# Weight blocks read in pieces of 16 KB instead of 2 KB, in a block of two transformer layers on one core

## The reference

```python
c_act = jax.nn.silu(c)
ada = c_act @ w_ada[l] + b_ada[l]              # w_ada: 1024 x 3072
shift, scale, gate = jnp.split(ada, 3, axis=-1)
h = rms_norm(x) * (1.0 + scale[:, None, :]) + shift[:, None, :]
p = h @ w_in[l]                                # w_in: 1024 x 3600
...
x = x + gate[:, None, :] * y
```

## Time and profile before

| | us |
|---|---|
| three runs | 2122.72, 2126.60, 2126.88 |
| median | 2126.6 |
| span of the profiled execution, first to last instruction | 2124.1 |
| PE busy in it | 2037.9 (96%) |
| PE busy in its first 60 us | 38.6 |

### The profile page before, as it was taken

How to read it: one execution, slowest core, us unless ns; L and a number is a source line. 1 busy time by engine, 2 the same in 40 slices (tenths; PEclk the granted TensorE clock), 3 DMA queues, 4 the chain that set the end, 5 groups by cost and what they waited for, 6 DMA issues and landing times.

```text
span 2124.1 us, 37932 instructions
## 1 busy us (share of the span) xinstructions
PE 2037.9 (96%) x15636; PEld 1158.4 (55%) x15636; DVE 915.3 (43%) x1510; ACT 573.6 (27%) x1048; POOL 326.1 (15%) x292
## 2 busy tenths in 40 slices
PE   6999999999999999999999999999899999999996
PEld 3486655655334445543456444565566666666653
DVE  2535551555556642886466554244611111111114
ACT  2123322333663210442133221143011111111113
POOL 0214430532330012004000010000100000000003
PEclk9999999999999999999999999999899999999999
DMA  8210311123104026100122102100899999999986
GB/s 317 86 45 25 105 60 60 70 85 104 40 8 151 30 90 153 71 1 0 40 80 81 68 0 80 43 31 40 319 384 410 413 410 411 405 403 410 400 359 244
DMA packets 108971, 346.90 MB, mean 163 GB/s; under 512 B 20216, under 2 KB 59536, under 8 KB 95952
## 3 DMA queue, kind: packets, MB, share of 16 engines
q1 hardware_dynamic: 64272, 274.98, 33.3%
q0 software_dynamic: 14528, 48.51, 6.8%
q10 hardware_dynamic: 30080, 22.18, 3.2%
HBM read 310.77 MB, written 40.24 MB: 165 GB/s over the span
## 4 chain that ended last, share of the span: by engine, by line
PE 86%; DVE 7%; ACT 4%; issue 1%; DMA 1%; POOL 1%; DVEq 0%; ACTq 0%; POOLq 0%; PEldq 0%
PE bank L685 19%; PE bank L1482 16%; PE bank L692 11%; PE bank L840 9%; PE bank L1498 8%; ACT work L1602 3%; PE bank L927 2%; PE bank L866 2%; PE bank L1263 1%; PE bank L1059 1%; PE bank L760 1%; PE bank L1488 1%; PE bank L1473 1%; DVE O L2115 1%; PE bank L1064 1%
## 5 line engine op out<-in xcount | busy, mean ns | idle before, releaser
L685 PE MATMUL bank<-slots,HT 128*128 128x512 f32 (+2 forms) x832 | 295.3, 511 | 1.7 <-DVEq L144 1.1
L1602 ACT ACTIVATE work<-bank 128x512 f32<-128x512 f32 (+6 forms) x227 | 117.4, 522 | 406.1 <-PE bank L685 120.0
L685 PEld LDWEIGHTS bank<-slots,HT 128*128 128x128 f32 x832 | 146.4, 190 | 134.0 <-issue 128.7
L1602 ACT ACTIVATE HT<-bank 64x256 f32<-64x256 f32 (+2 forms) x215 | 92.9, 432 | 433.0 <-PE bank L1482 278.4
L1602 ACT ACTIVATE work<-work 128x1024 f32<-128x1024 f32 (+7 forms) x199 | 158.6, 808 | 169.2 <-DVEq L144 114.4
L1482 PE MATMUL bank<-slots,HT 128*32 128x256 f32 x3136 | 172.4, 379 | 2.2 <-DVE HT L2862 1.3
L2868 DVE TENSOR_TENSOR HT<-HT,bank 64x256 f32<-64x256 f32 x97 | 41.0, 423 | 300.3 <-ACT HT L1602 300.3
L1482 PE MATMUL bank<-work,HT 128*32 128x256 f32 x3072 | 168.7, 379 | 0.0
L2982 POOL TENSOR_TENSOR work<-work 128x1024 f32<-128x1024 f32 (+4 forms) x80 | 120.3, 1504 | 240.8 <-DVEq L144 150.6
L1482 PEld LDWEIGHTS bank<-slots,HT 128*32 128x32 f32 x3136 | 103.1, 110 | 68.5 <-issue 2.9
L1482 PEld LDWEIGHTS bank<-work,HT 128*32 128x32 f32 x3072 | 101.1, 110 | 64.6
(11 more groups left out here) (319 smaller groups left out, 2922.5 us busy)
## 6 DMA issues: line engine op xcount, KB each, us to landing
slots<-in_w_e_gate_dram SPq DMA_DIRECT2D x17, 2048.0 KB, 11.1
slots<-in_w_e_up_dram SPq DMA_DIRECT2D x17, 2048.0 KB, 15.8
slots<-in_w_e_down_dram SPq DMA_DIRECT2D x17, 2048.0 KB, 17.2
work<-in_w_e_gate_dram SPq DMA_DIRECT2D x16, 2048.0 KB, 11.4
work<-in_w_e_up_dram SPq DMA_DIRECT2D x16, 2048.0 KB, 15.9
work<-in_w_e_down_dram SPq DMA_DIRECT2D x16, 2048.0 KB
slots<-in_w_in_dram SPq DMA_DIRECT2D x9, 2048.0 KB, 8.4
slots<-in_w_ada_dram SPq DMA_DIRECT2D x6, 2048.0 KB, 14.8
```

The source lines that it names most:

```text
L685: ins = pe.matmul(bank, lhsT, rhs, start=(n == 0), stop=(n == len(pairs) - 1))
L1602: return act.activation(o, i, f, bias=bias, scale=scale, **more)
```

## The change

The host lays out each block of 512 columns of `w_ada` so that each partition's part (8 row blocks of 512 floats) is one run of 16 KB, as it already does for the experts' weights, and does the same with a copy of the first 512 columns of `w_in`. The kernel loads `ada0` to `ada5` and `a_qk` from there. The place in `slots`, the bytes, the order, the waits and all products stay as they are. `w_in` itself stays as an input for the other blocks.

```diff
+def column_blocks(w, n=HALF):
+
+    return by_partition(np.stack([w[:, at:at + n] for at in range(0, w.shape[1], n)]))
...
-        w_ada, w_in, w_out = (A[n].rearrange("a (k p) n -> p (a k) n", p=P) for n in ("w_ada", "w_in", "w_out"))
+        w_in, w_out = (A[n].rearrange("a (k p) n -> p (a k) n", p=P) for n in ("w_in", "w_out"))
+        w_ada = [cut(A["w_ada"][n], NK) for n in range(6)]
...
         for n in (0, 2):
-            add_chunk(f"ada{n}", (w_ada, 512 * n, 512 * n + 512))
-        add_chunk("a_qk", (w_in, 0, 512))
+            add_chunk(f"ada{n}", (w_ada[n], 0, 512))
+        add_chunk("a_qk", (cut(A["w_in_first"][0], NK), 0, 512))
         for n in (1, 3):
-            add_chunk(f"ada{n}", (w_ada, 512 * n, 512 * n + 512))
+            add_chunk(f"ada{n}", (w_ada[n], 0, 512))
...
-        add_chunk("ada4", (w_ada, 512 * 4, 512 * 5))
+        add_chunk("ada4", (w_ada[4], 0, 512))
...
-        add_chunk("ada5", (w_ada, 512 * 5, 512 * 6))
+        add_chunk("ada5", (w_ada[5], 0, 512))
...
+    arrays["in_w_ada_dram"] = column_blocks(_np.asarray(inputs["w_ada"])[0])
+    arrays["in_w_in_first_dram"] = column_blocks(_np.asarray(inputs["w_in"])[0][:, 0:HALF])
```

More of the change, by code:

```diff
@@ L3316 @@
         arrays[f"in_{name}_dram"] = by_partition(_np.asarray(inputs[name])[0])
+    arrays["in_w_ada_dram"] = column_blocks(_np.asarray(inputs["w_ada"])[0])
+    arrays["in_w_in_first_dram"] = column_blocks(_np.asarray(inputs["w_in"])[0][:, 0:HALF])
     for name, table in zip(("consts", "masks", "packed"), (*constants(), packed(inputs))):
         arrays[f"in_{name}_dram"] = table
-    for name in _INS + ["consts", "masks", "packed"]:
+    for name in _INS + ["w_in_first", "consts", "masks", "packed"]:
         a = arrays[f"in_{name}_dram"]
```

## The result

The changed kernel took 2136.26 us (median of 4 runs, 2134.57 to 2138.82) against 2126.36 for the kernel before. The medians are 9.9 us apart. The ratio over all runs is 1.0052, with a 95% interval of 1.0039 to 1.0065, so by it the kernel is slower by some 11 us (8 to 14). The forecast was 2140.4, range 2133 to 2144. The profiled execution has a span of 2133.6 us, 9.5 more than before.

The account below looks back on a forecast made before the run. PE is busy 96%; early on the chain waits for x, not weights. 16 KB weight packets taking turns with x's 4 KB rows move ACT's pair 1 start from 15.40 to 29.2: 2126.6 + 13.8 = 2140.4 us, range 2133 to 2144.

Parts of the forecast that it names:

- rival A: `ada1` comes late and finds q1 empty, so x is through first: pair 1 at 23.9, +8.5 us, 2135.1; 16%.
- main case: x pair 1 lands at 29.2, behind the three first weight loads and `ada1`: +13.8 us, 2140.4, own range 2137 to 2143; 65%.
- Form and turns: The changed loads really get 16 KB packets, and the engines still take the queues one to one by packet.
- Rival B: x keeps at least half the bandwidth, as engines weigh bytes or cut 16 KB pieces: +1.1 us, 2127.7; 8%.
- x pair 0 near 19.6: x pair 0, 16 turns beside 16 KB packets, lands near 19.6 instead of 11.3.
- `ada0` landing near 8: `ada0` lands near 8 instead of 13.7, but its product waits for silu until about 16.5.
- The small transfers near 16.5, `ada1` issued near 20.1: q10's `packed` and identity land near 16.5, not 8.2; the product with `ada0` ends at 20.0, then SP issues `ada1`.
- `ada1` follows `a_qk` without a gap, pair 1 at 29.2: On q1 `a_qk` ends at 21.8, `ada1` starts near 22.0, ahead of x's last rows; pair 1 lands at 29.2: +13.8 us.
- Everything after hangs in one chain: All work after ACT's start on pair 1 shifts by the same 13.8 us; nothing later gives time back.
- Clock, priced at 0 within 1.6 us: PE's granted clock over the transposes, 0.69 after idleness, starts low again after a longer wait: 0, within 1.6 us.
- Rival C: A gain: x's first packet comes sooner or PE misses a 1.2 GHz stretch; ACT begins 3.3 us sooner, 2123.3; 3%.
- The page of the Trainium skill on small descriptors: Some three cycles of overhead per packet would bring the same bytes 3% sooner, under 1 us; rows showed no such gain.

Follow-up runs that it names:

- extra_load: Changed kernel with one more 2 MB load in 16 KB pieces issued right behind `a_qk`; 2142.10 us, ratio 1.0079 to the kernel before.
- hold_ada1: Changed kernel, but SP issues `ada1` only when x pair 1 has landed; 2134.04 us, ratio 1.0043 to the kernel before.
- pieces_2kb: Changed kernel's layout with 64 unused bytes after every 2 KB, so packets are 2 KB again; 2125.51 us, ratio 1.0002 to the kernel before.
- the additional products: 48 identity products on PE before its first real product, added to both x-first kernels; 2124.62 us (16 KB) and 2126.19 us (2 KB).
- x_first_16kb: Changed kernel, but SP issues x pairs 0 and 1 itself ahead of `ada0`; 2120.60 us, ratio 0.9978 to the kernel before; repeat 2120.07 us.
- x_first_2kb: Kernel before, with x pairs 0 and 1 moved to SP's queue ahead of `ada0`; 2125.80 us, ratio 1.0004 to the kernel before.

## Why the prediction was right, point by point

The direction and the mechanism were right: x loses its turns' worth of bandwidth to the longer packets, and the chain hands the delay on unchanged. One term of the sum was not, and it makes 4.3 us of 13.8: whether `ada1` follows `a_qk` at once. The measured 2136.26 lies inside 2133 to 2144 because that range took in rival A; the main case's own range, 2137 to 2143, begins 0.7 us above it.

- *Form and turns.* Right. 16 KB pieces are one packet, and q0 and q1 sent equal numbers of packets at 2, 4, 8 and 16 KB. Rival B, x keeping half of the bytes, would have given 2127.7. It is refuted by the 272 to 273 packets with 3.93 and 1.05 MB.
- *x pair 0 near 19.6.* It landed at 1.28 + 17.9 = 19.2, so near in part by luck: the engines moved 424 GB/s from 6 to 14 us and not the 400 of the earlier trace rows, and its 16 completions have a mean of 18.4, but the last of them came 0.8 us after that.
- *`ada0` landing near 8.* It landed at 9.7, and nothing waited for it.
- *The small transfers near 16.5, `ada1` issued near 20.1.* ACT started at 16.50, and SP issued at 20.20:

```profile
20.20 17.30 SPq L3238 DMA_DIRECT2D slots<-in_w_ada_dram  x2
```

- *`ada1` follows `a_qk` without a gap, pair 1 at 29.2.* This is the step that failed, and the term that was mis-sized by it. From 21 to 22 us, then from 22 to 23:

```profile
q0 software_dynamic: 85, 0.35, 85.6%
q1 hardware_dynamic: 15, 0.03, 8.5%
...
q0 software_dynamic: 101, 0.40, 98.8%
q1 hardware_dynamic: 5, 0.07, 15.7%
```

  The pieces of `a_qk` had begun by 21, all but two, and ended at 21.2 in the mean, not 21.8, since the engines moved 422 GB/s from 8 to 20 us and not the 395 to 400 that I had taken. The first piece of `ada1` began at 22.76, 2.5 us after the issue, not 1.9 after. Between 21.24 and 22.76 no piece began in q1, so x had the engines almost to itself, and from 21 to 23 it sent 186 packets, 0.75 MB. Of the 128 pieces of `ada1`, all of which I had put ahead of x's last rows, 31 had begun by 24. Pair 1 started at 24.86 instead of 29.2, and +13.8 became +9.5. Rival A, at 16%, had this step right (`ada1` finds q1 empty, x is nearly through first, +8.5), but not what brings it about: the small transfers were not late. I had left a margin of 0.2 us (21.8 to 22.0), and errors of 0.6 and 0.8 us on its two sides opened the gap. extra_load closes it and gives 15.5, hold_ada1 keeps `ada1` out altogether and gives 8.9.
- *Everything after hangs in one chain.* Right: 9.46, 9.60, 9.68 and 9.5 us at four points down to the end.
- *Clock, priced at 0 within 1.6 us.* The transposes took 5.42 us instead of 5.28. In the experiments they took from 3.71 to 6.57, within the 1.6 us. But the bound left out the first terms, which took 12.02 before and from 10.57 to 13.42 in the experiments; in the changed kernel both together cost 0.22.
- *Rival C* (an earlier start of x) did not occur: 2 packets of q0 from 4 to 6 us, where the earlier trace rows have 10.
- *The page of the Trainium skill on small descriptors* (DMA: Bandwidth & Descriptors, Why small descriptors are slow) has some three cycles of overhead for each packet; by my estimate from it 2 KB packets lose about 4% and 16 KB under 1%. I had set it aside by the earlier trace rows. From 6 to 14 us the engines moved 400 GB/s before and 404 with pieces_2kb, and 413, 425 and 424 with 4, 8 and 16 KB. So the trace leans its way, with 6% where the estimate has 3%, and `a_qk` being through 0.6 us early was part of the error above. Why have only 395 with 16 KB stays open.

## What to carry to other kernels

Where two queues shared the DMA engines here, they sent equal numbers of packets at 2, 4, 8 and 16 KB, so each got bandwidth in proportion to its packet size, and a longer contiguous run sped up its own transfer (`ada0` in 9.0 us instead of 13.0) at the cost of what stood beside it (x pair 1 in 22.7 instead of 13.0). Before lengthening one, ask which of the transfers in flight the first compute waits for. What is needed first can go first in the same queue, where it waits for no turn: with x there, it was in by 9 us with either size, the large pieces did no harm, and the kernel came out 0.22% ahead of the one before. With 2 KB the same move gained nothing, so that it pays by itself is not shown. Sum such a delay to the last engine and not to the mean (with pieces of 4 KB and more, the last completion of pair 1 came 0.6 to 1.2 us after the mean of the 16), and look for gaps in the competing queue, in which the small packets catch up.

## What was not expected of the hardware

- For their size the small transfers suffer most. 137 KB on ACT's queue landed at 16.5 us instead of 8.2, since each of their packets, of 584 or 512 bytes, waits for its turn beside one of 16 KB: from 10 to 12 us q1, q0 and q10 sent 42, 44 and 44 packets. With 4 and 8 KB pieces ACT could start at 7.81 and 8.86, and with pieces_2kb at 5.99, so below 16 KB their landing varies as much between kernels as with the size.
- The granted clock of PE in the first 45 us differed between kernels in which the same work falls at other times. By their profiles, the first terms took 12.02 us before, 13.42 with x first and 2 KB, 10.57 in both profiles of x first and 16 KB, and with the additional products 12.26 (16 KB) and 10.57 (2 KB); the transposes took 3.71 to 6.57. x_first_16kb showed the higher clock in both of its profiles and was 5 us faster than x_first_2kb, of which the earlier start explains 0.6 us. What makes the clock stay up there remains open, and so does how much of the 5 us it accounts for.
